# Expert products in two streams of different width, 64 columns for eight experts and 2 x 32 for the other pairs

## What is computed

```python
N_GROUPS, EXPERTS_PER_GROUP, TOP_K = 4, 8, 2     # 32 experts
D_MODEL, D_EXPERT = 1024, 256

def hier_moe(h, w_group, b_group, w_router, b_router, w_gate, w_up, w_down):
    pg = jax.nn.softmax(hf @ w_group + b_group, axis=-1)
    g_val, g_idx = lax.top_k(pg, 1)
...
    e_val, e_idx = lax.top_k(pe, TOP_K)
    expert = g_idx * EXPERTS_PER_GROUP + e_idx
...
    a = jnp.einsum('btd,edf->btef', h, w_gate)
    u = jnp.einsum('btd,edf->btef', h, w_up)
    z = jax.nn.silu(a) * u * combine[..., None].astype(a.dtype)
    return jnp.einsum('btef,efd->btd', z, w_down).astype(h.dtype)
```

## Time and profile before

| | |
|---|---|
| three runs, median (lowest to highest) | 679.55 us (678.01 to 680.33) |
| profiled execution: time | 675.53 us |
| profiled execution: span | 673.7 us |
| mean granted clock of TensorE | 0.909 of full speed |
| TensorE, weight loads, DVE, ACT, POOL busy | 80%, 41%, 34%, 23%, 27% of the span |
| HBM read, written | 165.18 MB, 18.32 MB |

### The profile page before, as it was taken

One profiled execution on the slowest core, in us unless ns is written; L12 is line 12 of the kernel. 1 busy time (PEld: TensorE's weight loads), 2 busy tenths in 40 slices (PEclk: granted clock), 3 DMA queues, 4 the chain that ended last, 5 costly groups with the idle time before them and its releaser, 6 DMA issues.

```text
span 673.7 us, 7215 instructions
## 1 busy us (share of the span) xinstructions
PE 540.6 (80%) x2420; PEld 273.9 (41%) x2421; DVE 230.5 (34%) x530; ACT 151.7 (23%) x312; POOL 179.0 (27%) x204
## 2 busy tenths in 40 slices
PE   1879999999889799662069999989999979789460
PEld 0467777886433344322023333333333423233220
DVE  0432444325394486876101111111111101011295
ACT  1222344516373012210011111111111101011021
POOL 4020010000554443662621122112112111111075
PEclk9969999999799899975569999999999979799685
DMA  8992946203818611118459968349999999995611
GB/s 283 407 365 105 342 159 229 88 1 117 327 76 340 206 62 63 62 41 324 202 188 401 421 281 317 138 180 419 421 419 421 418 421 420 417 372 198 254 60 68
DMA packets 46005, 168.98 MB, mean 251 GB/s; under 512 B 13178, under 2 KB 22450, under 8 KB 30590
## 3 DMA queue, kind: packets, MB, share of 16 engines
q1 hardware_dynamic: 36682, 146.48, 55.3%
q0 software_dynamic: 8944, 21.87, 9.1%
q10 hardware_dynamic: 340, 0.09, 0.1%
HBM read 165.18 MB, written 18.32 MB: 272 GB/s over the span
## 4 chain that ended last, share of the span: by engine, by line
PE 60%; DVE 15%; DMA 9%; SPq 6%; issue 5%; ACT 3%; POOL 1%; POOLq 0%; DVEq 0%
PE B L1665 18%; PE B L1417 15%; PE B L1684 8%; DMA wex<-in_w_up 4%; PE B L1581 3%; PE B L1354 3%; SPq L370 2%; DMA x_tok<-in_x_sample 2%; PE B L1486 2%; DVE bn L1140 2%; SPq L372 1%; SPq L369 1%; DVE yy L1322 1%; PE B L1646 1%; PE B L1672 1%
## 5 line engine op out<-in xcount | busy, mean ns | idle before, releaser
L1665 PE MATMUL B<-wex,XT 128*64 128x512 f32 x640 | 150.7, 620 | 17.5 <-DMA wex<-in_w_up 9.9
L1417 PE MATMUL B<-hT,win 128*128 128x256 f32 (+1 forms) x448 | 104.1, 393 | 2.1 <-DVE hT L963 2.1
L1665 PEld LDWEIGHTS B<-wex,XT 128*64 128x64 f32 x640 | 52.5, 143 | 113.7 <-issue 112.5
L1417 PEld LDWEIGHTS B<-hT,win 128*128 128x128 f32 x448 | 86.2, 195 | 22.6 <-issue 9.5
L1684 PE MATMUL B<-wex,zT 128*64 128x512 f32 x320 | 73.1, 598 | 0.6
L1295 DVE TENSOR_TENSOR z<-silu_g,B 128x256 f32<-128x256 f32 x20 | 8.4, 421 | 161.1 <-ACT silu_g L853 161.1
L622 POOL COPY sidx<-idx_all 128x1 int32 (+1 forms) x20 | 3.6, 181 | 198.9 <-DVE yo L1300 198.9
L1581 PE MATMUL B<-wout,yT 128*128 128x512 f32 x112 | 50.1, 606 | 0.0
L1646 PE MATMUL B<-ident,X 128*128 128x128 f32 x168 | 28.4, 294 | 26.6 <-DMA X<-h_dram,gidx 26.6
L1300 DVE COPY yo<-B 128x512 f32<-128x512 f32 x20 | 13.8, 692 | 83.1 <-PE B L1684 83.1
L853 ACT ACTIVATE silu_g<-B 128x256 f32<-128x256 f32 x20 | 7.7, 385 | 153.0 <-PE B L1665 153.0
(11 more groups left out here) (324 smaller groups left out, 631.4 us busy)
## 6 DMA issues: line engine op xcount, KB each, us to landing
wex<-in_w_gate SPq DMA_DIRECT2D x32, 1024.0 KB, 16.9
wex<-in_w_up SPq DMA_DIRECT2D x32, 1024.0 KB, 19.6
wex<-in_w_down SPq DMA_DIRECT2D x32, 1024.0 KB, 21.0
ada<-in_w_ada POOLq DMA_DIRECT2D x12, 1024.0 KB, 7.2
ada<-in_w_ada SPq DMA_DIRECT2D x8, 1024.0 KB, 7.2
win<-in_w_in SPq DMA_DIRECT2D x7, 1024.0 KB, 13.3
wout<-in_w_out SPq DMA_DIRECT2D x1, 4096.0 KB, 13.3
yy<-y_dram SPq DMA_DIRECT2D x8, 512.0 KB, 7.1
```

The source lines that it names most:

```text
L1417: last = pe.matmul(B[(q % 2) * 2 + h][:, 0:cn], win[:, n % 3, k, col:col + P], hT[:, k, c0:c0 + cn], start=(k == 0), stop=(k == KD - 1))
L1665: last = pe.matmul(B[2 + j % 2][64 * q:64 * q + 64, :], XT[:, j % 2, k, 64 * q:64 * q + 64], gu[:, :, k, :], start=(k == 0), stop=(k == KD ...
```

## The change

**Steps.** A step now holds 64 columns of one expert of group 0 (experts 0 to 7, stream A, 8 units) beside 32 columns each of the two experts of a pair of the other 24 (stream B, 12 units). The two streams count their units apart (`uend`), and the loop has as many steps as the longer stream; both streams are computed in every step.

**Weights.** Stream A has two buffers of one expert, stream B two buffers of one pair, in the same memory as the three sets before. SP loads them in one written order, `LOADS`. Of stream B one pair and a half are loaded ahead of the loop, and the rest of the second pair waits for the second gather.

**Rings and control.** The rings of `X` and `yo` are two deep (four before), and the rows are gathered two steps ahead. A turn is two steps. TensorE has four arms for each, one for each combination of buffers, and a single loop of `TURNS` turns with a test before each step. `TURNS` is now 22, from a bound of 44 steps. The other engines run six turns without a test and then test each step. POOL loads four register values before it signals.

**Routing.** DVE works out the two streams' numbers apart; a row's shift and slot stride depend on its group. `y_v` and `y_a` are one higher throughout, so that the first step needs no case of its own.

```diff
-CAP = 64
-NPAIR = NE // 2
-MAXSTEP = (2 * NT + (CAP - 1) * NPAIR) // CAP
-RING = 4
-AHEAD = RING - 1
+NA, NB = EPG, (NE - EPG) // 2
+NU = NA + NB
+WA, WB = 64, 32
+MAXSTEP = max((2 * NT + (WA - 1) * NA) // WA, (2 * NT + (WB - 1) * NB) // WB)
+RING = 2
+AHEAD = 2
 TURNS = (MAXSTEP + RING - 1) // RING
-MINTURNS = NPAIR // RING
+MINTURNS = max(NA, NB) // RING
 NSTEP = RING * TURNS + RING
...
-        SETS = 3
-        wex = [row("wex0", [P, 2, EXW], "r", 0), row("wex1", [P, 2, EXW], "r", 8 * EXW), row("wex2", [P, 2, EXW], "x", 0)]
+        wA = [row("wA0", [P, 1, EXW], "r", 0), row("wA1", [P, 1, EXW], "r", 4 * EXW)]
+        wB = [row("wB0", [P, 2, EXW], "x", 0), row("wB1", [P, 2, EXW], "r", 8 * EXW)]
...
+        LOADS = [("A", 2), ("B", 2), ("A", 3), ("B", 3), ("B", 4), ("A", 4), ("B", 5), ("A", 5), ("B", 6), ("B", 7),
+                 ("A", 6), ("B", 8), ("A", 7), ("B", 9), ("B", 10), ("B", 11)]
...
-            sp.wait_ge(lgT_ps, 2)
-            load_expert(2, 1, 0)
+            sp.wait_ge(x1_stored, 16 * (TT + 1))
+            load_b(0, 0)
+            load_b(0, 1)
             sp.wait_ge(lg_ps, 1)
             sp.wait_ge(h2_stored[0], 16 * (TT // 2 + 1))
             sp.wait_ge(h2_stored[1], 16 * (TT // 2))
-            load_expert(3, 1, 1)
-            sp.wait_ge(x1_stored, 16 * (TT + 1))
-            load_expert(4, 2, 0, (True, False))
+            load_b(1, 0)
             sp.wait_ge(X_in[AHEAD - 1], 16)
-            load_expert(4, 2, 0, (False, True))
-            load_expert(5, 2, 1)
+            load_b(1, 1)
...
+            for kind, i in LOADS:
+                before = (i - 2) if kind == "A" else NA + i - 2
+                last_step = sp.value_load(uend_i[0:1, before:before + 1], min_val=1, max_val=MAXSTEP)
                 for half, done in enumerate((gu_ps, y_ps)):
                     sp.wait_ge(done, last_step)
-                    for q in range(2):
-                        load_expert(2 * SETS * i + (2 * j + q), j, q, (half == 0, half == 1))
-            with sp.Fori(1, NPAIR // SETS) as i:
-                for j in range(SETS):
-                    load_pair(i, j)
-            for j in range(NPAIR % SETS):
-                load_pair(NPAIR // SETS, j)
-            last_step = sp.value_load(pend_i[0:1, NPAIR - 2:NPAIR - 1], min_val=1, max_val=MAXSTEP)
+                    parts = (half == 0, half == 1)
+                    if kind == "A":
+                        load_a(i, parts)
+                    else:
+                        load_b(i, 0, parts)
+                        load_b(i, 1, parts)
...
+            step(dve.tensor_scalar(unum_i[:, 0, 0:NA], B[5][:, 0:NA], 1.0, float(WA - 1), ALU.max, ALU.add))
+            link(dve.tensor_reduce(umax[:, NA:NU], B[5][:, NA:NE].rearrange("p (a b) -> p a b", b=2), AX.X, ALU.max))
+            link(dve.tensor_scalar(unum_i[:, 0, NA:NU], umax[:, NA:NU], 1.0, float(WB - 1), ALU.max, ALU.add))
+            step(dve.tensor_scalar(unum_i[:, 1, 0:NA], unum_i[:, 0, 0:NA], 6, None, ALU.arith_shift_right))
...
+            in_a = gt[:, 2, :, 0:1].broadcast_to((P, TT + 1, 2))
+            step(dve.tensor_scalar(shift_i[:, :, :], in_a, 1.0, 5.0, ALU.mult, ALU.add))
+            step(dve.tensor_scalar(wide[:, :, :], in_a, float((WB - WA) * NSTEP), float(1 - WB * NSTEP), ALU.mult, ALU.add))
...
-            def turn(i, peeled):
-                for j in range(RING):
-                    s = RING * i + j
-                    if not (peeled and j == 0):
-                        pool.wait_ge(XT_ps, counted(2 * s))
-                    gather((j + AHEAD) % RING, s + AHEAD, AHEAD + 2 * s)
-                    scatter(j, s)
+            def one(i, j):
+                s = RING * i + j
+                pool.wait_ge(XT_ps, counted(2 * s + 2))
+                gather((j + AHEAD) % RING, s + AHEAD, AHEAD + 2 * s)
+                scatter(j, s)
             for s in range(AHEAD):
                 gather(s, s, s)
-            turn(0, True)
+            for j in range(RING):
+                one(0, j)
             with pool.Fori(1, MINTURNS) as i:
-                turn(i, False)
+                for j in range(RING):
+                    one(i, j)
             pool.wait_ge(steps_ready, 1)
-            nturns = pool.value_load(turns[0:1, 0:1], min_val=MINTURNS, max_val=TURNS)
+            nsteps = pool.value_load(steps_i[0:1, 0:1], min_val=RING * MINTURNS, max_val=MAXSTEP)
             with pool.Fori(MINTURNS, TURNS) as i:
-                with pool.If(nturns > i):
-                    turn(i, False)
-            scattered, gathered = counted(16 * nturns, 16 * nturns + 16)
+                for j in range(RING):
+                    with pool.If(nsteps > RING * i + j):
+                        one(i, j)
...
+            ends = [pool.value_load(more_i[0:1, 0, j:j + 1], min_val=16 * MINTURNS, max_val=16 * (TURNS + 2)) for j in range(2 * RING)]
             for j in range(RING):
-                pool.wait_ge(y_out[j], scattered)
-                pool.wait_ge(X_in[j], gathered if j < AHEAD else scattered)
-            pool.memset(mark[:, :], 0.0).then_inc(experts_done, 1)
+                pool.wait_ge(y_out[j], ends[j])
+                pool.wait_ge(X_in[j], ends[RING + j])
+            pool.tensor_tensor(mark[:, :], mark[:, :], mark[:, :], ALU.add).then_inc(experts_done, 1)
...
+            def lanes(a, b):
+                return [(0, WA, wA[a][:, 0, :]), (WA, WB, wB[b][:, 0, :]), (WA + WB, WB, wB[b][:, 1, :])]
+            def one(i, j):
+                n = RING * i + j
+                arm = pe.value_load(arm_i[0:1, bass.ds(n, 1)], min_val=0, max_val=3)
+                need_a = pe.value_load(wneed[0:1, 0, bass.ds(n, 1)], min_val=32, max_val=16 * NA)
+                need_b = pe.value_load(wneed[0:1, 1, bass.ds(n, 1)], min_val=64, max_val=32 * NB)
+                for a in range(2):
+                    for b in range(2):
+                        with pe.If(arm == 2 * a + b):
                             pe.wait_ge(XT_v, n + 1)
                             pe.wait_ge(XT_a, n + 1)
-                            pe.wait_ge(w_in[pl], need)
+                            pe.wait_ge(wA_in[a], need_a + ADA)
+                            pe.wait_ge(wB_in[b], need_b + ADA)
                             for k in range(KD):
-                                for q in range(2):
-                                    gu = wex[pl][:, q, 0:GU].rearrange("p (c k f) -> p c k f", c=2, k=KD)
-                                    last = pe.matmul(B[2 + j % 2][64 * q:64 * q + 64, :], XT[:, j % 2, k, 64 * q:64 * q + 64],
+                                for c0, cn, w in lanes(a, b):
+                                    gu = w[:, 0:GU].rearrange("p (c k f) -> p c k f", c=2, k=KD)
+                                    last = pe.matmul(B[2 + j % 2][c0:c0 + cn, :], XT[:, j % 2, k, c0:c0 + cn],
                                                      gu[:, :, k, :], start=(k == 0), stop=(k == KD - 1))
                             last.then_inc(gu_ps, 1)
...
-                            if not (peeled and j == 0):
-                                pe.wait_ge(y_v, n)
-                                pe.wait_ge(y_a, n)
-                            pe.wait_ge(down_in[pl], need_down)
+                            pe.wait_ge(y_v, n + 1)
+                            pe.wait_ge(y_a, n + 1)
+                            pe.wait_ge(dA_in[a], need_a)
+                            pe.wait_ge(dB_in[b], need_b)
                             for k in range(2):
                                 for c in range(2):
-                                    for q in range(2):
-                                        dn = GU + k * D + c * 512
-                                        last = pe.matmul(B[5 + c][64 * q:64 * q + 64, :], zT[:, k, 64 * q:64 * q + 64],
-                                                         wex[pl][:, q, dn:dn + 512], start=(k == 0), stop=(k == 1))
+                                    dn = GU + k * D + c * 512
+                                    for c0, cn, w in lanes(a, b):
+                                        last = pe.matmul(B[5 + c][c0:c0 + cn, :], zT[:, k, c0:c0 + cn],
+                                                         w[:, dn:dn + 512], start=(k == 0), stop=(k == 1))
                             last.then_inc(y_ps, 1)
...
-            turn(0, True)
-            with pe.Fori(1, MINTURNS) as i:
-                turn(i, False)
-            nturns = pe.value_load(turns[0:1, 0:1], min_val=MINTURNS, max_val=TURNS)
-            with pe.Fori(MINTURNS, TURNS) as i:
-                with pe.If(nturns > i):
-                    turn(i, False)
+            nsteps = pe.value_load(steps_i[0:1, 0:1], min_val=RING * MINTURNS, max_val=MAXSTEP)
+            with pe.Fori(0, TURNS) as i:
+                for j in range(RING):
+                    with pe.If(nsteps > RING * i + j):
+                        one(i, j)
```

(39 more changed lines are left out.)

181 lines of the change are left out of this document (81 added, 100 removed).

## The result

The changed kernel takes 810.6 us (median of 4 runs, 809.6 to 811.7) where the kernel before takes 679.1: ratio 1.193, 95% interval 1.190 to 1.195. The forecast was 807 us. Its profiled execution took 810.5 us with a span of 808.5, beside the 673.7 of before: 134.8 us more.

What follows compares the result with a forecast made beforehand. TensorE bound, weight stream close behind. Span: 345.7 + 391.5 + 2.2 = 739.4, + 51.4 present rest + 10.5 tail = 801.3 us, 127.6 more; with the median 4.0 above the profiled time, 807 us, range 760 to 865.

Steps and rivals of the forecast that it cites:

- Two widths in a slice drain TensorE: Expert products: 64- and 32-column runs never overlap; slice 2.01 us for 0.86, step 26.1 us, fifteen 391.5; 78%.
- The term of 0.14 to 0.15 us for a change of width: Expert products: each run of one width pays some 0.15 us for the change of width.
- The fast rival: Expert loop: three tiles overlap, mixed slice under about 1.3 us, step 12.5 us, weights bound the loop; 658 us; 13%.
- The code rival: TensorE's four longer arms: each step pays a 2.3 us issue wait, 35 us in all, 842 us; 5%.
- Start of the loop: First step of the expert loop: begins at the lower clock, 9.24 against 7.09 us, +2.2 us.
- Routing: DVE before the first gather: about five more small operations and one more linked one, +0.7 us (bounds 0 and 1.2).
- Tail: After the last step: POOL skips 14 turns and loads registers before signalling; 15.8 us copy to read, +10.5 us.
- The other engines skip too: Tail: the other engines' skipped turns add nothing, since DVE's masks are wanted only with SP's reads of the results.
- No wait for weights: Expert loop: up to three experts a step, 22.9 us of loading, hidden under a 26.1 us step; DMA waits end.

Runs made afterwards that it cites:

- the grouped order: Changed kernel with each step's 64-column products all before its 32-column ones, for gate/up and for down; 779.6 us, ratio 1.149.
- the 655.1 us version: Changed kernel with four 32-column tiles, TensorE's loop of one step ending at the step count, idle turns passed at once, arm found by two tests; 655.1 us, ratio 0.966.
- the short loop: TensorE's loop cut from two steps to one, four arms for eight, against the changed kernel: four tiles of 32 took 690.3 us, mixed widths 816.6 us.
- the 690.3 us version: Changed kernel with four tiles of 32 columns and TensorE's loop cut to one step and four arms; 690.3 us, ratio 1.018.

## Why the prediction was right

**Two widths in a slice drain TensorE: right, and so was its size.** Forecast 2.01 us a slice, measured 1.99; step 26.1, measured 25.81, over 15 steps 4 us less. The term of 0.14 to 0.15 us for a change of width measured 0.13 in the grouped order. Three experiments separate it from the rest: two widths share no time even in long blocks, the old kernel with mixed widths shows the same 15.9 and 8.0 us, and without the narrow tiles the change is 154 us faster. The Trainium skill (TensorEngine Tiling (Array Packing), Key Properties) says that changing the tiling mode drains the engine; the trace agrees, 1.99 us a slice for 0.86. The section gives no price.

**The fast rival.** Its condition failed; its price is borne out by the version with two tiles of 64: 658 us with the weights as bound and the loop's end at 590, measured 656.9 and 594.6. That the 655.1 us version lies there too is no support, since its tail is some 10 us shorter than the rival's (51.6 us behind the last copy for 51.4 + 10.5).

**The code rival was mis-shaped.** It was put as the largest present issue wait, 2.3 us, in every step. The changed kernel paid none of that: its waits are 2.3 and 9.3 us, before the first and the second step, and the second has two tests of 3.8 and 5.8 us in it while the loop's code was fetched for the first time. The real cost is another shape: no later wait with 1,312 records in the loop, 207.5 us with 1,696. The forecast did not ask for this size, so that the change stayed on the near side was luck. The Trainium skill (Runtime: NRT & Kernel Launch, Instruction fetch mechanics) says that a taken branch beyond a window of two pages waits for a fetch; the loops of before and after disagree, with 18 and 6 packets over all their branches and, in the changed kernel, no test above 0.21 us from 403 us on. The same section gives TensorE room for 2,048 instructions. The records leave out branches and register work, some 30 in a step of the trace with four tiles of 32; at most 8 x (212 + 30), an estimate of some 1,900 for its loop, so the edge measured here seems to lie a little below that.

**Start of the loop: mis-sized, the largest miss.** "+2.2" counted one gate/up pass at the lower clock. Two were (18.58 and 18.45 against 15.90: 5.2 us), and before the second stood the 9.3 us of issue wait. Together 12.3 us more than forecast. The loop came to 402.0 us, of which 15 x 25.8 = 387.2.

**Routing.** The first product began at 346.4, forecast 345.7.

**Tail: right, a little too large.** Forecast 15.8 us from copy to read, measured 14.5; everything behind the copy 60.2 us against 51.4, +8.8 for the +10.5. "The other engines skip too" was costed at nothing because DVE's masks are wanted only with the reads; that held while GpSimd was later, and with GpSimd's turns gone it became the next term at once, 11.0 us for DVE.

**No wait for weights.** Right: none in the loop. The sum: -4.3 (steps) + 12.3 (start of the loop) + 0.7 (routing) - 1.7 (tail) = +7.0 on the forecast span of 801.3, measured 808.5. The forecast time then added 4.0 us because the profiled execution of before lay that far below its median; the changed kernel's lies 0.1 below. So the span was 7 us off and the time only 3.6, by luck.

## What to carry to other kernels

Before cutting TensorE's tiles by load, look whether every tile in flight has one width: two widths take turns, here 1.99 us where equal tiles took 0.86, and no order of the products mends it. Count what a loop's unrolled copies and arms hold before adding products to them: here code was fetched only on a loop's first pass at 1,392 records, and at 1,696 throughout, for 207.5 us of waits. It is seen in the instruction queue's packets and in the length of the branches, not in any engine's work. When a skip loop is taken off one engine's tail, look at the others', since the next can stand right behind: here 9.5 us taken off GpSimd gave 3.6.

## What was not expected of the hardware

- A TensorE loop of 1,392 recorded operations keeps its code after one pass, and one of 1,696 fetches it again and again: 4 to 26 us before each step but the first, 67 packets of 16 KB in 15 steps.
- With four tiles of 32, 96 records of expert products a step, some 2.3 us of issue wait stand before each step in the short loop, where the earlier trace rows has 0.48, and some 1.7 us with two tests in place of four. With two tiles of 64 columns it is at most 0.8, and with mixed widths in the short loop 0 to 0.8. This fits a sequencer that gets no lead over the array when products are many and short, so that the tests and register loads of a step stand bare; no run isolates it.
- A 2.28 us wait of this kind was followed by a gate/up pass at a mean granted clock of 0.81, one of 1.77 us by a pass at 1.00. The wait's length alone does not decide: in the 690.3 us version the passes behind 2.13 and 2.45 us took 7.11 us, as at full clock, and the one behind 1.97 us took 8.92. What decides is open.
